# Where the modulation rows of two FFN layers stand in the instruction order: out of the gate/value tail and the down projection, into slots between the weight splits of the up projection

## The chip, the core and the metric

The kernel runs on one NeuronCore of a Trainium2 chip. The metric is the device time of one execution in microseconds (us). The engines of the core run their own instruction streams in order and meet at semaphores only: TensorE (PE) multiplies, VectorE (DVE) and ScalarE (ACT) do the elementwise work, GpSimd (POOL) helps, SyncE (SP) issues the transfers from HBM.

## The reference, cut to what matters

The program is a whole two-part network on 512 positions of width 1024. The first part has two layers, each a mixer and a convolutional FFN. The second part is modulated by a conditioning vector:

```python
def conv_ffn(x, w_up, conv_w, conv_b, w_down):          # D_FF = 2816
    gate, val = jnp.split(x @ w_up, 2, axis=-1)
    gp = jnp.pad(gate, ((0, 0), (CONV_WIDTH - 1, 0), (0, 0)))
    conv = conv_b
    for j in range(CONV_WIDTH):                          # 3 taps
        conv = conv + conv_w[j] * gp[:, j:j + s_]
    return (jax.nn.silu(conv) * val) @ w_down
...
# second part, layer i
shift, scale, gate = jnp.split((silu_c @ ada_w[i] + ada_b[i])[:, None, :], 3, axis=-1)
shift_c, scale_c, gate_c = jnp.split(silu_cc @ ada_w[i] + ada_b[i], 3, axis=-1)
```

`silu_c @ ada_w[i]` is a vector (1024) times a matrix (1024 x 3072). It depends on none of the first part's activations, so the kernel computes it beside the two FFNs: the modulation of second-part layer 0 (for two vectors, `silu_c` and `silu_cc`) beside `ffn(0)`, that of layer 1 (for one vector) beside `ffn(1)`.

## The kernel before, in words

All activations lie with the features on the 128 partitions and the 512 positions along the free axis. Weights come as one stream of chunks of 128 x 1024 floats, which are 8 tiles of 128 x 128. SP loads a chunk into one of 4 buffers `raw`. ACT rounds it to `whi` (L1176), DVE computes the rest `wlo = raw - whi` (L1780), each into one of 3 buffers. A projection multiplies each tile three times, `whi` by the high part, `whi` by the low part, `wlo` by the high part of the activation (L318, L321, L322). PE starts a chunk when its `wlo` is there (semaphore `w_lo`). ACT may write the `whi` of chunk c once PE has started chunk c - 1, because the buffer is that of chunk c - 3 and PE frees a chunk with the first matmul of the next (`w_used`).

An FFN has 22 feature blocks f, worked in two halves of 11. For each f, PE runs a gate projection (8 tiles, so one chunk, 24 matmuls) and a value projection (one chunk, 24 matmuls). DVE makes two `wlo` chunks per f and then does `tail(f)`: `gp` (L2045, out of PSUM), two convolution steps (L2049, L2052), the value (L2055), two products (L2057, L2060) and `hl` (L2064), the low part of the hidden block. ACT has a step between `gp` and L2049 (L1338), one after L2052 (a tanh, L1341) and one between L2060 and `hl` (L1345). Both engines' order is fixed by the program: the chunk splits (class `Ahead`) run up to two chunks ahead of the chunk that the program is at. DVE therefore makes in iteration f the `wlo` of the gate and the value of f + 1, in the order `wlo`, `wlo`, `tail(f)`.

After 11 blocks PE runs the down projection of that half: 8 output blocks of 11 tiles. Tile k of the first output block waits for `hl` of the k-th hidden block of the half.

The modulation is a generator `ada(layer)` on PE and one on DVE. It is advanced by `next(ad, None)` calls that stand between other work, so the number and the places of these calls and of the `yield`s in it set the order. The matrix comes as 24 rows of 128 x 1024 floats, `KD * g + k`, for three groups g of 8. For each row SP loads `aw` (3 buffers in layer 0, 2 in layer 1), and DVE adds `aw` times a scalar to `col` (L1998 for k = 0, L1995 else), twice per row in layer 0 (two vectors) and once in layer 1. After a group of 8 rows PE sums `col` over the partitions with 16 (layer 0) or 8 (layer 1) matmuls of one column each (L536) into bank 6. At the end DVE adds the bias (L2004) and forms the gains. `tiles.mark` in PE's generator sets where in the weight stream SP issues the load of a row.

In `ffn(1)` a second generator, `context()`, runs after `tail(f)` of f = 12 to 19: DVE multiplies a block of the context (L2027, left to POOL for k = 1, 4, 7), ACT shifts and rounds it, and DVE subtracts (L2029).

Of the kernel before, what the change touches and what calls it, by code (L numbers as in the profile page):

```python
# [13 lines left out]
MUL, ADD, SUB = ALU.mult, ALU.add, ALU.subtract  # L14
# [3 lines left out]
KD = 8  # L18
# [4 lines left out]
AW = 3, 2  # L23
# [69 lines left out]
def run(gen):  # L93
    for _ in gen:
        pass
# [180 lines left out]
HG_TILES = [0, 0, 3, 2, 2, 2, 2, 2, 2, 2, 1, 1, 1, 3, 0, 1]  # L276
MLA_BANKS = [{"tr0": 7, "tr1": 4, "qn": 5, "kn": 7, "knc": 4, "sg": 5}, {"qn": 7, "kn": 4, "knc": 5, "sg": 7}]
MLA_OUT_BANKS = [7, 4, 5, 3, 0, 1, 2, 6]
HIDDEN_AT = {(3, 2): 0, (4, 2): 1, (5, 2): 2}


# [27 lines left out]
def tensor_program(e, m, s):  # L309
    q = Waits(e)  # L310
    tiles = Tiles(q, s, m)
# [210 lines left out]
    def ada(layer):  # L522

        nv = 2 - layer
        b, col = B[6], m.ffn[layer].col
        for g in range(3):
            for k in range(KD):
                tiles.mark(("ada", layer, KD * g + k))
                yield
            q.wait_ge(*s.made_v.at("col", layer, nv - 1, KD * g + KD - 1))  # L530
            if g == 0:
                q.wait_ge(*(s.hid_lo.at("on", KD - 1) if layer else s.taken_v.at("o", KD - 1)))
            for v in range(nv):
                for j in range(8):
                    at = nv * (8 * g + j) + v
                    op = e.matmul(b[:, at:at + 1], col[:, v, 128 * j:128 * j + 128], ones[:, 0:1], start=True, stop=True)  # L536
            op.then_inc(*s.filled.tick("ada", layer, g))
            yield

    def ffn(layer):  # L540
        a = m.ffn[layer]
        site = ("n1", "n3")[layer]
        up, dn = f"up{layer}", f"down{layer}"
        hh, hl = [a.hh[:, i, :] for i in range(HF)], [a.hl[:, i, :] for i in range(HF)]
        before = ("w_out", "wo")[layer]
        ready0 = operands_ready(site)
        ad = ada(layer)

        def bank_free(half, f, j):
            b = (2 * f + j) % 6  # L550
            if f > half * HF + 2:
                return lambda: q.wait_ge(*s.taken_v.at("gv"[j], layer, f - 3))
            if half:
                return lambda: q.wait_ge(*s.h.at(dn, 0, {0: 6, 1: 7}.get(b, b)))
            if b < 4:
                return lambda: q.wait_ge(*s.h.at(before, 4 + b))
            if layer == 0:
                return lambda: q.wait_ge(*(s.made_v.at("S", KD - 1, 2) if b == 4 else s.taken_v.at("o", KD - 2)))
            return lambda: q.wait_ge(*s.made_a.at("pt", KD - 1, 2 + b - 4))

        def behind(f, j):
            if j == 0 and f == 0:
                return {7: summed(site, rb_read(("o", KD - 1)) if layer == 0 else lambda: q.wait_ge(*s.h.at("wo", 0)))}
            if j == 1 and f == 0:
                return {5: spread(site)}
            if layer == 1 and j == 0 and f == 11:
                def ready():
                    q.wait_ge(*s.acc.at("ctx", KD - 1))
                    q.wait_ge(*s.rb.at("n3"))
                return {3: sums("ctx", m.acc, 2, ready), 7: spread("ctx", n=2)}  # L570
            return {}

        for half in range(2):
            for f in range(half * HF, half * HF + HF):
                run(project(2 * f % 6, up, f, ("gate", layer, f), nhi, nlo, bank_free(half, f, 0),
                            ready0 if f == 0 else nothing, then=behind(f, 0)))
                run(project((2 * f + 1) % 6, up, FT + f, ("val", layer, f), nhi, nlo, bank_free(half, f, 1),
                            then=behind(f, 1)))
                if f > 1:
                    next(ad, None)  # L580

            def ready(k, half=half):
                q.wait_ge(*s.hid_lo.at("f", layer, half * HF + k))

            for i in range(KD):
                f0 = half * HF + HF - 3

                def free(i=i, f0=f0):
                    if i >= 6:
                        q.wait_ge(*s.h.at(dn, half, i - 6))  # L590
                        return
                    for f in range(f0, f0 + 3):
                        for j in range(2):
                            if (2 * f + j) % 6 == i:
                                q.wait_ge(*s.taken_v.at("gv"[j], layer, f))
                run(project(i % 6, dn, i, (dn, half, i), hh, hl, free, ready, ks=HF, k0=half * HF))
                if half == 0:
                    next(ad, None)

    def swa():  # L600
        a = m.swa
# [529 lines left out]

    hgrn()
    ffn(0)
    swa()
    ffn(1)
    mla()
    hyena()
# [635 lines left out]
def vector_program(e, m, s, chunks):  # L1773
    q = Waits(e)
# [205 lines left out]
    def ada(layer):  # L1980
        nv = 2 - layer
        ad, gs = m.ada[layer], m.gs[layer]
        bias = par[:, PC[f"ada_b{layer}"]:PC[f"ada_b{layer}"] + 24].unsqueeze(2).to_broadcast((128, 24, nv))
        col, aw = m.ffn[layer].col, m.ffn[layer].aw

        for g in range(3):
            for k in range(KD):
                n = KD * g + k
                q.wait_ge(*s.ada_w[n % AW[layer]].at(layer, n))
                if k == 0 and g:  # L1990
                    q.wait_ge(*s.filled.at("ada", layer, g - 1))
                for v in range(2):
                    if v < nv and k:
                        q.wait_ge(*s.made_v.at("col", layer, v, n - 1))
                        e.scalar_tensor_tensor(col[:, v, :], aw[:, n % AW[layer], :], m.scv[:, 2, k, v:v + 1], col[:, v, :],  # L1995
                                               MUL, ADD).then_inc(*s.made_v.tick("col", layer, v, n))
                    elif v < nv:
                        e.tensor_scalar(col[:, v, :], aw[:, n % AW[layer], :], m.scv[:, 2, k, v:v + 1], None,  # L1998
                                        MUL).then_inc(*s.made_v.tick("col", layer, v, n))
                    yield  # L2000
            yield
            yield
        q.wait_ge(*s.filled.at("ada", layer, 2))
        e.tensor_tensor(ad[:, 0:24, 0:nv], B[6][:, 0:24 * nv].rearrange("p (m v) -> p m v", v=nv), bias,  # L2004
                        ADD).then_inc(*s.ada_o.tick(layer))
        gain = par[:, PC[f"norm_g{layer}"]:PC[f"norm_g{layer}"] + 8].unsqueeze(2).to_broadcast((128, KD, nv))
        q.wait_ge(*s.ada_o.at(layer))
        e.tensor_scalar(gs[:, :, 0:nv], ad[:, 8:16, 0:nv], 1.0, None, ADD).then_inc(*s.setup_v.tick("gs1", layer))
        q.wait_ge(*s.setup_v.at("gs1", layer))
        e.tensor_tensor(gs[:, :, 0:nv], gs[:, :, 0:nv], gain, MUL).then_inc(*s.setup_v.tick("gs2", layer))  # L2010
        if layer == 0:
            q.wait_ge(*s.setup_v.at("gs2", 0))
            e.tensor_tensor(gs[:, :, 0], gs[:, :, 0], par[:, PC["final_norm"]:PC["final_norm"] + 8],
                            MUL).then_inc(*s.setup_v.tick("gs3"))
# [17 lines left out]
    def ffn(layer):  # L2032
# [5 lines left out]
        ad = ada(layer)  # L2038
        side = context() if layer else iter(())

        def tail(f):
# [1 line left out]
            q.wait_ge(*s.filled.at("gate", layer, f))  # L2043
            q.wait_ge(*s.rb.at(site))
            e.tensor_tensor(gp[:, z, 2:T + 2], B[2 * f % 6], m.rb[:, :], MUL).then_inc(*s.taken_v.tick("g", layer, f))  # L2045
            if f > 1:
                next(ad, None)
            q.wait_ge(*s.made_a.at("c0", layer, f))
            e.scalar_tensor_tensor(t[:, 2, z, :], gp[:, z, 1:T + 1], pc(cw, 22 + f), t[:, 0, z, :], MUL,  # L2049
                                   ADD).then_inc(*s.made_v.tick("c1", layer, f))  # L2050
# [7 lines left out]
                                   MUL).then_inc(*s.made_v.tick("s2", layer, f))  # L2058
            q.wait_ge(*s.made_v.at("s2", layer, f))
            e.tensor_tensor(t[:, 3, z, :], t[:, 0, z, :], t[:, 3, z, :], MUL).then_inc(*s.made_v.tick("mo", layer, f))  # L2060
            if f > 1:
                next(ad, None)
            q.wait_ge(*s.hid_hi.at("f", layer, f))
            e.tensor_tensor(a.hl[:, i, :], t[:, 3, z, :], a.hh[:, i, :].bitcast(F),  # L2064
                            SUB).then_inc(*s.hid_lo.tick("f", layer, f))
# [1 line left out]
        for half in range(2):  # L2067
            for f in range(half * HF, half * HF + HF):
                for k in range(KD):
                    w.tiles(1)  # L2070
                    if f == 0 and k == 7:
                        root(site, m.rc)
                    if layer and f == 11 and k == 3:
                        root("ctx", a.rcc, 2)
                if f == 1:
                    tail(0)
                run(w.steps(KD))
                if f:
                    tail(f)
                if f > 1:  # L2080
                    next(side, None)
            for i in range(KD):
                run(w.steps(HF))
                if half == 0:
                    next(ad, None)
                    next(ad, None)
                residual(i % 6, i, (dn, half))
                if half and layer == 0:
                    lo_scaled("n2", i, pc("attn_norm", i))
# [851 lines left out]
```

## Time and profile before

| quantity | us |
|---|---|
| median of 3 runs (2130.52 to 2132.89) | 2131.46 |
| the profiled execution's own time | 2130.52 |
| its span, first to last instruction | 2128.7 |
| PE busy | 2032.9 |
| DVE busy | 1360.7 |
| ACT busy | 807.0 |

The profiled execution is the fastest of the three. 1.8 us of its own time lie outside the span. The mean granted TensorE clock is 0.984 of full speed. Matmuls overlap in their pipeline, so their listed durations (about 390 ns) are longer than the distance from one to the next; the starts in a timeline tell how fast PE goes.

### The profile page before, as it was taken

The page shows a single profiled execution, that of the slowest core. Times are in us where ns is not written, and L with a number is a line of the kernel's source. Part 1 is how long each engine was busy: PE and PEld are TensorE (multiplying, and loading weights), DVE is VectorE, ACT ScalarE, POOL GpSimd, SP SyncE. Part 2 cuts the span into 40 slices and gives each one's busy share as a digit, 9 for nine tenths or more (in the row PEclk, how much of TensorE's full clock was granted, in tenths as well). Part 3 has the DMA queues.
Part 4 walks back from the last instruction along what each step waited for, and adds up shares of the span by engine and source line. Part 5 has one row for each costly group of instructions (what it writes and reads, how often), then busy time and mean ns, then how long its engine had stood idle before and what let it go on. Part 6 is the DMA issues. An engine that isn't in the chain of part 4 may idle for free.

```text
span 2128.7 us, 24442 instructions
## 1 busy us (share of the span) xinstructions
PE 2032.9 (95%) x9814; PEld 1657.6 (78%) x9814; DVE 1360.7 (64%) x1937; ACT 807.0 (38%) x1236; POOL 234.2 (11%) x239
## 2 busy tenths in 40 slices
PE   8999999999999989999999999999999799999887
PEld 6888887888888878888888887777776576768676
DVE  4577766875684566567648745544445678787774
ACT  4333334331333445444324434333333343444342
POOL 2133321000000100100000011000001213120201
PEclk9999999999999999999999999999999899999998
DMA  5211113434332300234443323111001222233221
GB/s 183 71 50 51 59 50 100 158 121 159 132 128 83 104 31 31 70 137 148 150 139 129 119 89 109 50 40 40 31 30 62 82 73 94 79 105 100 74 89 50
DMA packets 55009, 191.61 MB, mean 90 GB/s; under 512 B 6000, under 2 KB 6320, under 8 KB 54768
## 3 DMA queue, kind: packets, MB, share of 16 engines
q1 hardware_dynamic: 54896, 190.04, 26.6%
q8 instruction: 78, 1.28, 0.2%
q14 instruction: 35, 0.29, 0.0%
HBM read 187.92 MB, written 2.10 MB: 89 GB/s over the span
## 4 chain that ended last, share of the span: by engine, by line
PE 76%; DVE 15%; ACT 5%; issue 2%; POOL 2%; DMA 0%; SPq 0%; DVEq 0%; ACTq 0%
PE PS L318 20%; PE PS L322 19%; PE PS L321 19%; DVE wlo L1780 2%; PE PS L430 2%; PE PS L890 2%; PE PS L864 2%; PE PS L865 2%; PE PS L325 2%; PE PS L328 2%; PE PS L329 2%; ACT s_s L1406 1%; PE PS L879 1%; PE PS L380 1%; DVE s_s L2117 1%
## 5 line engine op out<-in xcount | busy, mean ns | idle before, releaser
L318 PE MATMUL PS<-nhi,whi 128*128 128x512 f32 x1456 | 601.4, 413 | 25.4 <-DVE nlo L1817 8.5
L322 PE MATMUL PS<-nhi,wlo 128*128 128x512 f32 x1456 | 574.0, 394 | 0.0
L321 PE MATMUL PS<-nlo,whi 128*128 128x512 f32 x1456 | 573.3, 394 | 0.0
L1780 DVE TENSOR_TENSOR wlo<-raw,whi 128x1024 fp32r<-128x1024 f32 x291 | 361.7, 1248 | 231.5 <-ACT whi L1176 230.9
L1176 ACT ACTIVATE whi<-raw 128x1024 fp32r<-128x1024 f32 x291 | 304.2, 1052 | 197.7 <-PE PS L318 180.7
L318 PEld LDWEIGHTS PS<-nhi,whi 128*128 128x128 f32 x1456 | 277.3, 190 | 97.2 <-issue 18.4
L322 PEld LDWEIGHTS PS<-nhi,wlo 128*128 128x128 f32 x1456 | 276.8, 190 | 60.5
L321 PEld LDWEIGHTS PS<-nlo,whi 128*128 128x128 f32 x1456 | 277.6, 191 | 52.9 <-issue 2.6
L2578 POOL TENSOR_TENSOR diag<-diag,sqb 128x512 f32<-128x512 f32 (+1 forms) x56 | 73.3, 1309 | 1175.3 <-ACT sqb L1185 1092.9
L318 PE MATMUL PS<-hh_f,whi 128*128 128x512 f32 x352 | 138.2, 393 | 0.0
L322 PE MATMUL PS<-hh_f,wlo 128*128 128x512 f32 x352 | 137.9, 392 | 0.0
L321 PE MATMUL PS<-hl_f,whi 128*128 128x512 f32 x352 | 137.9, 392 | 0.0
L1824 DVE TENSOR_TENSOR hT<-hT,PS 128x512 f32<-128x512 f32 x48 | 32.9, 685 | 92.7 <-PE PS L322 92.7
L1560 ACT ACTIVATE pt_m<-PS 128x768 f32<-128x768 f32 x32 | 26.0, 813 | 157.5 <-PE PS L879 157.5
L1995 DVE SCALAR_TENSOR_TENSOR col_f<-aw_f,scv,col_f 128x1024 f32<-128x1024 f32 x63 | 79.9, 1277 | 0.0
L318 PEld LDWEIGHTS PS<-hh_f,whi 128*128 128x128 f32 x352 | 66.8, 190 | 14.0
L322 PEld LDWEIGHTS PS<-hh_f,wlo 128*128 128x128 f32 x352 | 66.6, 189 | 14.0
L321 PEld LDWEIGHTS PS<-hl_f,whi 128*128 128x128 f32 x352 | 66.7, 189 | 13.8
L2291 DVE TENSOR_REDUCE sm_m<-PS 128x1 f32<-128x768 f32 x32 | 30.6, 956 | 62.9 <-PE PS L865 62.9
L1338 ACT ACTIVATE t_f<-gp_f,par 128x512 f32<-128x512 f32 x44 | 35.9, 817 | 85.4 <-DVE gp_f L2045 85.4
L430 PEld LDWEIGHTS PS<-qa,kk 128*128 128x128 f32 x448 | 56.0, 191 | 14.3 <-DVE qa L1932 10.3
L1185 ACT ACTIVATE sqb<-hT 128x512 f32<-128x512 f32 x42 | 26.3, 629 | 107.0 <-DVE hT L1824 70.3
(344 smaller groups left out, 3360.0 us busy)
## 6 DMA issues: line engine op xcount, KB each, us to landing
raw<-in_stream SPq DMA_DIRECT2D x291, 512.0 KB, 3.5
aw_f<-in_ada SPq DMA_DIRECT2D x48, 512.0 KB, 4.4
dc<-in_decay SPq DMA_DIRECT2D x4, 1024.0 KB, 5.5
hT<-in_xT SPq DMA_DIRECT2D x8, 256.0 KB, 7.3
out<-hT SPq DMA_DIRECT2D x8, 256.0 KB, 2.0
ctx_f<-in_ctx SPq DMA_DIRECT2D x1, 1024.0 KB, 6.8
ab_h<-in_filt_out SPq DMA_DIRECT2D x8, 128.0 KB, 2.9
mask<-in_masks SPq DMA_DIRECT2D x1, 512.0 KB, 8.7
```

Source lines behind the costliest of these rows:

```text
L318: op = e.matmul(out, hi, xh, start=first, stop=False)
L321: e.matmul(out, hi, xl, start=False, stop=False)
L322: return e.matmul(out, lo, xh, start=False, stop=last)
L325: op = e.matmul(out, xh, w[0], start=first, stop=False, skip_group_check=skip)
L328: e.matmul(out, xh, w[1], start=False, stop=False, skip_group_check=skip)
L329: return e.matmul(out, xl, w[0], start=False, stop=last, skip_group_check=skip)
L430: op = e.matmul(B[b][:, cs], kk[:, z, cs], qx[:, cs], start=True, stop=True)
L864: e.matmul(b[:, 0:n], a.qn[:, z, c], a.kn[:, z, ks], start=True, stop=False)
L1176: e.activation(m.whi[:, c % HL, :], m.raw[:, c % RAW, :], ACT.Copy).then_inc(*s.w_hi.tick(c))
L1780: e.tensor_tensor(m.wlo[:, c % HL, :], m.raw[:, c % RAW, :], m.whi[:, c % HL, :].bitcast(F), SUB).then_inc(*s.w_lo.tick(c))
L1995: e.scalar_tensor_tensor(col[:, v, :], aw[:, n % AW[layer], :], m.scv[:, 2, k, v:v + 1], col[:, v, :], MUL, ADD).then_inc(*s.made_v.tick(" ...
L2578: e.tensor_tensor(acc, acc, m.sqb[:, i % 2 if site != "n4" else 0, 0:width], ADD).then_inc(*s.acc.tick(site, i))
```

## The change

The rows of the modulation are placed by a table, `ADA_AT`, of 12 slots per group, of which 8 hold a row. Both generators now begin with three empty slots. In the up projection there are two slots per f (one in f = 0), the first behind the gate projection, the second behind the value projection. The slots inside `tail(f)` and in the down projection are gone. In layer 0 a slot of DVE now holds both vectors of a row.

```diff
+ADA_AT = [None, None, 0, 1, 2, 3, None, 4, 5, 6, 7, None]
...
         b, col = B[6], m.ffn[layer].col
+        for _ in range(3):
+            yield
         for g in range(3):
-            for k in range(KD):
-                tiles.mark(("ada", layer, KD * g + k))
+            for k in ADA_AT:
+                if k is not None:
+                    tiles.mark(("ada", layer, KD * g + k))
                 yield
             q.wait_ge(*s.made_v.at("col", layer, nv - 1, KD * g + KD - 1))
...
             op.then_inc(*s.filled.tick("ada", layer, g))
-            yield
...
                 run(project(2 * f % 6, up, f, ("gate", layer, f), nhi, nlo, bank_free(half, f, 0),
                             ready0 if f == 0 else nothing, then=behind(f, 0)))
+                next(ad, None)
                 run(project((2 * f + 1) % 6, up, FT + f, ("val", layer, f), nhi, nlo, bank_free(half, f, 1),
                             then=behind(f, 1)))
-                if f > 1:
+                if f:
                     next(ad, None)
...
-                if half == 0:
-                    next(ad, None)
...
+        for _ in range(3):
+            yield
         for g in range(3):
-            for k in range(KD):
...
-                    yield
-            yield
-            yield
+            for k in ADA_AT:
+                if k is not None:
+                    row(g, k)
+                yield
+        yield
         q.wait_ge(*s.filled.at("ada", layer, 2))
...
             e.tensor_tensor(gp[:, z, 2:T + 2], B[2 * f % 6], m.rb[:, :], MUL).then_inc(*s.taken_v.tick("g", layer, f))
-            if f > 1:
-                next(ad, None)
...
             e.tensor_tensor(t[:, 3, z, :], t[:, 0, z, :], t[:, 3, z, :], MUL).then_inc(*s.made_v.tick("mo", layer, f))
-            if f > 1:
-                next(ad, None)
...
                 if f == 1:
                     tail(0)
+                next(ad, None)
                 run(w.steps(KD))
                 if f:
+                    next(ad, None)
                     tail(f)
...
                 run(w.steps(HF))
-                if half == 0:
-                    next(ad, None)
-                    next(ad, None)
                 residual(i % 6, i, (dn, half))
```

`row(g, k)` holds the waits and the one or two DVE instructions of a row, unchanged. The placement of both versions, the same in both layers:

| | group 0 | group 1 | group 2 |
|---|---|---|---|
| before: rows | one per f, f = 2 to 9 | one per output block of the first down projection | one per f, f = 12 to 19 |
| before: PE's one-column matmuls | behind f = 10 | behind f = 11 | behind f = 20 |
| after: rows | f = 3 to 7 (2, 2, 1, 2, 1) | f = 9 to 13 (2, 2, 1, 2, 1) | f = 15 to 19 (2, 2, 1, 2, 1) |
| after: PE's one-column matmuls | in f = 8, behind the gate | in f = 14, behind the gate | in f = 20, behind the gate |

On DVE in layer 0, one iteration of f (here f = 4). `wlo` is a weight split, `col_f` the modulation, `gp_f` to `hl_f` the tail. Before:

```order
L2064 TENSOR_TENSOR hl_f<-t_f,hh_f 128x512
L1780 TENSOR_TENSOR wlo<-raw,whi 128x1024 x2
L2045 TENSOR_TENSOR gp_f<-PS,rb 128x512
L1995 SCALAR_TENSOR_TENSOR col_f<-aw_f,scv,col_f 128x1024
L2049 SCALAR_TENSOR_TENSOR t_f<-gp_f,par,t_f 128x512
L2052 SCALAR_TENSOR_TENSOR t_f<-gp_f,par,t_f 128x512
L2055 TENSOR_TENSOR t_f<-PS,rb 128x512
L2057 SCALAR_TENSOR_TENSOR t_f<-t_f 128x512
L2060 TENSOR_TENSOR t_f<-t_f 128x512
L1995 SCALAR_TENSOR_TENSOR col_f<-aw_f,scv,col_f 128x1024
L2064 TENSOR_TENSOR hl_f<-t_f,hh_f 128x512
```

The same iteration after, where it holds two rows of the matrix:

```order
L1782 TENSOR_TENSOR wlo<-raw,whi 128x1024
L1997 SCALAR_TENSOR_TENSOR col_f<-aw_f,scv,col_f 128x1024 x2
L1782 TENSOR_TENSOR wlo<-raw,whi 128x1024
L1997 SCALAR_TENSOR_TENSOR col_f<-aw_f,scv,col_f 128x1024 x2
L2052 TENSOR_TENSOR gp_f<-PS,rb 128x512
L2054 SCALAR_TENSOR_TENSOR t_f<-gp_f,par,t_f 128x512
L2057 SCALAR_TENSOR_TENSOR t_f<-gp_f,par,t_f 128x512
L2060 TENSOR_TENSOR t_f<-PS,rb 128x512
L2062 SCALAR_TENSOR_TENSOR t_f<-t_f 128x512
L2065 TENSOR_TENSOR t_f<-t_f 128x512
L2067 TENSOR_TENSOR hl_f<-t_f,hh_f 128x512
```

Four `col_f` instructions stand in front of `gp_f` where two stood inside the tail, and none stands between `gp_f` and the first convolution step or in front of `hl_f` any more.

On PE in layer 0, the change from the up projection of the first half (operand `nhi`) to the down projection (operand `hh_f`). Before:

```order
L318 MATMUL PS<-nhi,whi 128x512
L321 MATMUL PS<-nlo,whi 128x512
L322 MATMUL PS<-nhi,wlo 128x512
L536 MATMUL PS<-ones,col_f 128x1 x16
L318 MATMUL PS<-hh_f,whi 128x512
```

The group of one-column matmuls after, now in the middle of f = 8:

```order
L319 MATMUL PS<-nhi,whi 128x512
L322 MATMUL PS<-nlo,whi 128x512
L323 MATMUL PS<-nhi,wlo 128x512
L540 MATMUL PS<-ones,col_f 128x1 x16
L319 MATMUL PS<-nhi,whi 128x512
L322 MATMUL PS<-nlo,whi 128x512
```

It left the boundary between the two projections and stands between a gate and a value projection.

On DVE in layer 1, around a context step (`tmc_f`, `call`) in the second half. Before:

```order
L2064 TENSOR_TENSOR hl_f<-t_f,hh_f 128x512
L2027 TENSOR_TENSOR tmc_f<-ctx_f,rbc_f 128x256
L2029 TENSOR_TENSOR call<-tmc_f,call 128x256
L1780 TENSOR_TENSOR wlo<-raw,whi 128x1024 x2
L2045 TENSOR_TENSOR gp_f<-PS,rb 128x512
L1995 SCALAR_TENSOR_TENSOR col_f<-aw_f,scv,col_f 128x1024
L2049 SCALAR_TENSOR_TENSOR t_f<-gp_f,par,t_f 128x512
```

After, in an iteration with two rows:

```order
L2067 TENSOR_TENSOR hl_f<-t_f,hh_f 128x512
L2034 TENSOR_TENSOR tmc_f<-ctx_f,rbc_f 128x256
L2036 TENSOR_TENSOR call<-tmc_f,call 128x256
L1782 TENSOR_TENSOR wlo<-raw,whi 128x1024
L1997 SCALAR_TENSOR_TENSOR col_f<-aw_f,scv,col_f 128x1024
L1782 TENSOR_TENSOR wlo<-raw,whi 128x1024
L1997 SCALAR_TENSOR_TENSOR col_f<-aw_f,scv,col_f 128x1024
L2052 TENSOR_TENSOR gp_f<-PS,rb 128x512
L2054 SCALAR_TENSOR_TENSOR t_f<-gp_f,par,t_f 128x512
```

Here too the row left the place behind `gp_f`, and a second row joined it.

## Rows read from the trace of the kernel before

**Rows 1.** The page's chain of waits by engine, and PE's waits from 343 to 700 us

```profile
PE 76%; DVE 15%; ACT 5%; issue 2%; POOL 2%; DMA 0%; SPq 0%; DVEq 0%; ACTq 0%
...
PE PS L318 <- DVE nlo L1800: 0.2, 1, 0.2
```

**Rows 2.** Busy time of the engines (PE, PEld, DVE, ACT, POOL) in the first up projection

```profile
343.00:464.00 121.00, 120.79 (x548) 100.04 (x547) 96.47 (x119) 46.61 (x59) 0.06 (x1) 1.00 0.40 140
```

**Rows 3.** Timeline of DVE, layer 0, f = 5: start, duration, instruction, idle time before it

```profile
402.29 1.23 DVE L1780 TENSOR_TENSOR wlo<-raw,whi 128x1024 fp32r<-128x1024 f32 x1 [1.36 <-ACT whi L1176]
403.43 0.68 DVE L2045 TENSOR_TENSOR gp_f<-PS,rb 128x512 f32<-128x512 f32 x1
404.03 1.27 DVE L1995 SCALAR_TENSOR_TENSOR col_f<-aw_f,scv,col_f 128x1024 f32<-128x1024 f32 x1
405.22 0.74 DVE L2049 SCALAR_TENSOR_TENSOR t_f<-gp_f,par,t_f 128x512 f32<-128x512 f32 x1
...
409.99 0.68 DVE L2064 TENSOR_TENSOR hl_f<-t_f,hh_f 128x512 fp32r<-128x512 f32 x1
...
414.31 0.69 DVE L2045 TENSOR_TENSOR gp_f<-PS,rb 128x512 f32<-128x512 f32 x1
```

**Rows 4.** Timeline of DVE, layer 0, f = 1 to 2, without modulation

```profile
362.89 0.68 DVE L2045 TENSOR_TENSOR gp_f<-PS,rb 128x512 f32<-128x512 f32 x1
364.46 0.75 DVE L2049 SCALAR_TENSOR_TENSOR t_f<-gp_f,par,t_f 128x512 f32<-128x512 f32 x1 [0.89 <-ACT t_f L1338]
...
368.82 0.69 DVE L2064 TENSOR_TENSOR hl_f<-t_f,hh_f 128x512 fp32r<-128x512 f32 x1 [0.70 <-ACT hh_f L1345]
369.77 2.36 DVE L1780 TENSOR_TENSOR wlo<-raw,whi 128x1024 fp32r<-128x1024 f32 x2 [0.26 <-ACT whi L1176]
372.05 0.68 DVE L2045 TENSOR_TENSOR gp_f<-PS,rb 128x512 f32<-128x512 f32 x1
```

**Rows 5.** Timeline of DVE, two modulation rows (both vectors) in the down projection

```profile
468.11 1.41 DVE L1998 TENSOR_SCALAR col_f<-aw_f,scv 128x1024 f32<-128x1024 f32 x2
...
476.81 2.48 DVE L1995 SCALAR_TENSOR_TENSOR col_f<-aw_f,scv,col_f 128x1024 f32<-128x1024 f32 x2
```

**Rows 6.** Timeline of PE at one-column groups and in the down projection, layer 0

```profile
460.55 4.32 PE L536 MATMUL PS<-ones,col_f 128*128 128x1 f32 x32
...
474.19 0.39 PE L318 MATMUL PS<-hh_f,whi 128*128 128x512 f32 x1
...
538.11 3.63 PE L536 MATMUL PS<-ones,col_f 128*128 128x1 f32 x32
541.60 0.62 PE L318 MATMUL PS<-nhi,whi 128*128 128x512 f32 x1
```

**Rows 7.** Timeline of DVE at the ends and starts of halves, layer 0

```profile
463.74 0.69 DVE L2064 TENSOR_TENSOR hl_f<-t_f,hh_f 128x512 fp32r<-128x512 f32 x1 [0.69 <-ACT hh_f L1345]
...
535.39 0.68 DVE L2045 TENSOR_TENSOR gp_f<-PS,rb 128x512 f32<-128x512 f32 x1
...
551.50 0.69 DVE L2045 TENSOR_TENSOR gp_f<-PS,rb 128x512 f32<-128x512 f32 x1
```

**Rows 8.** Timeline of DVE, layer 1, second half, f = 11, 15 and 16

```profile
1104.75 0.68 DVE L2045 TENSOR_TENSOR gp_f<-PS,rb 128x512 f32<-128x512 f32 x1
...
1150.80 0.68 DVE L2045 TENSOR_TENSOR gp_f<-PS,rb 128x512 f32<-128x512 f32 x1
...
1160.04 2.36 DVE L1780 TENSOR_TENSOR wlo<-raw,whi 128x1024 fp32r<-128x1024 f32 x2 [0.34 <-ACT whi L1176]
1162.31 0.68 DVE L2045 TENSOR_TENSOR gp_f<-PS,rb 128x512 f32<-128x512 f32 x1
...
1170.35 2.36 DVE L1780 TENSOR_TENSOR wlo<-raw,whi 128x1024 fp32r<-128x1024 f32 x2 [0.53 <-ACT whi L1176]
```

**Rows 9.** Busy share by microsecond (PE, PEld, DVE, ACT, POOL), granted clock, DMA share, GB/s

```profile
465.00:466.00 1.00, 1.00 (x3) 0.81 (x3) 0.00 (x0) 0.12 (x1) 0.00 (x0) 0.50 0.00 0
...
770.00:771.00 1.00, 0.00 (x0) 0.00 (x0) 0.17 (x1) 0.99 (x4) 0.00 (x0) 1.00 0.00 0
```

More of the change, by code:

```diff
@@ L1984, in ada, with row @@
         col, aw = m.ffn[layer].col, m.ffn[layer].aw
-        for g in range(3):
-            for k in range(KD):
[L1988 to L1999, printed above, removed]
-                    yield
-            yield
-            yield
+        def row(g, k):
+            n = KD * g + k
+            q.wait_ge(*s.ada_w[n % AW[layer]].at(layer, n))
+            if k == 0 and g:
+                q.wait_ge(*s.filled.at("ada", layer, g - 1))
+            for v in range(nv):
+                c = m.scv[:, 2, k, v:v + 1]
+                if k:
+                    q.wait_ge(*s.made_v.at("col", layer, v, n - 1))
+                    op = e.scalar_tensor_tensor(col[:, v, :], aw[:, n % AW[layer], :], c, col[:, v, :], MUL, ADD)
+                else:
+                    op = e.tensor_scalar(col[:, v, :], aw[:, n % AW[layer], :], c, None, MUL)
+                op.then_inc(*s.made_v.tick("col", layer, v, n))
+        for _ in range(3):
+            yield
+        for g in range(3):
+            for k in ADA_AT:
[3 more added lines that the diff above has]
+        yield
         q.wait_ge(*s.filled.at("ada", layer, 2))
```

## The prediction

> **What bounds the kernel now.** I read the chain of waits first: three quarters of it is PE, and from 343 to 700 us, which is all of `ffn(0)`, PE waited 0.2 us [rows 1]. Then the busy times of an up projection: PE has 120.8 of 121 us, DVE 96.5 [rows 2]. So PE is the bound, and DVE has 20% to spare. How much of that a rearrangement may use is told by DVE's timeline. In steady state one f takes 10.88 us from `gp` to `gp` [rows 3], which is PE's pace for 48 matmuls (0.2267 each). DVE idles 1.36 us of it, and this idle is all that it has in front of a weight split. The `col` instructions cost little there, since they stand where DVE would wait for ACT: without them it idles 0.89 us behind `gp` and 0.70 us in front of `hl` [rows 4], with them it idles at neither place [rows 3]. The reader is to see both timelines side by side: the tail from `gp` to the end of `hl` takes 6.62 us without and 7.24 us with two `col` [rows 3, 4], so two instructions of 1.27 us cost 0.62 us.
>
> **What is removed, and what moved instructions cost.** No instruction is added or removed; the order shows them moved, so a change that does nothing is out. I keep two clocks. DVE's, when it runs behind: 9.16 us per f without modulation (372.05 - 362.89, [rows 4]), plus what stands in the new slots, where nothing of ACT's is hidden. A row of both vectors is 2.39 there (2.48 less 0.09 of overlap: a `col` starts 1.19 before its successor though it lasts 1.27, [rows 3]), the first of a group 1.33 [rows 5]. So an f with two rows takes 13.94 us, with one 11.55, with none 9.16, against PE's 10.88. Six f with eight rows need 9.16 x 6 + 1.33 + 7 x 2.39 = 73.0 us; PE needs 65.3 and 3.49 for the one-column group (541.60 - 538.11, [rows 6]), 68.8. So in layer 0 DVE becomes the bound of the up projection.
>
> How long PE doesn't notice: the next gate's `wlo` is the first thing behind a tail, done 8.2 us after `gp` (6.62, 0.26 idle, one split, [rows 4]). In steady state PE starts gate f at 13.6 us after `gp` of f - 2: gate 10 starts at 460.55 - 10.88 = 449.67 [rows 6], `gp` of f = 8 at 414.31 + 21.76 = 436.07 [rows 3]. The difference, 5.4 us, is what `gp` may be late.
>
> **Layer 0, first half.** From `gp` of f = 2 at 372.05 the sums give 384.9, 398.9, 410.4, 424.4, 435.9, 445.1, 458.0 and 471.9 for f = 3 to 10 (two rows, two, one, two, one, none, 1.33 + 2.39, two). The pace of before is 381.67 + 10.88 per f, so lateness is 3.3, 6.3, 7.0, 10.1, 10.7, 9.0, 11.0, 14.1. Gate 6 waits 0.9, gate 7 brings it to 1.6, gate 8 to 4.7; there the one-column group follows, so gates 9 and 10 wait no more. The end of the half binds harder. Tile 10 of the first down block needs `hl` of f = 10, that is 471.9 + 6.6 = 478.5, and a semaphore: 478.6. Before, `hl` was there at 464.4 [rows 7] and PE reached this tile at 474.19 (the 31st triple behind the group, [rows 6]), with 3.4 us lost to a low clock on the way (460.55 + 3.49 + 30 x 0.2267 = 470.8 without it). What the clock does in f = 8 now doesn't count, since `hl` is later anyway. Cost: **+4.4**.
>
> **Layer 0, second half.** `gp` of f = 11 stands at 535.39 before [rows 7]; one row in front makes it 2.4 late. Then 5.5 (f = 12), 6.1, 0.9 in f = 14, where the group gives DVE 3.5 us, 2.4 (its own row at least), 5.5, 6.1, 9.2 in f = 18, 9.9. Gate 20 waits 9.2 - 5.4 = 3.8; behind it stands the third group, which covers f = 19's lateness. `gp` 21 is 3 to 4 late, less than PE by now. Cost: **+3.8**.
>
> **Layer 1, first half.** One `col` per row, 1.20 in a slot and 0.7 for the first of a group. Two rows make 11.56, one 10.36: lateness 1.4, 2.1, 1.6, 2.2, 1.7, 0, 1.2, 1.9. Nothing over 5.4, and `hl` of f = 10 has 2.9 us before the down tile wants it (as in layer 0: 460.55 + 6.8 - 464.43, [rows 6, 7]). Cost: **0**.
>
> **Layer 1, second half.** Here the context step stands behind the tail. It makes f take 11.52 from f = 15 to 16 and 10.3 from 16 to 17, where POOL has its part (1162.31 - 1150.80 and 1170.35 + 2.27 - 1162.31, [rows 8]), with one `col` inside the tail, which adds 0.22 (half of a pair that hides nearly as well; 11.30 and 10.09 without). The next gate's split is done 10.5 us after `gp` with a full context step (1160.04 + 1.2 - 1150.80), 9.3 without, so slack is 3.1 or 4.3. From 1104.75 + 1.2 for f = 11 [rows 8]: lateness 1.2, 1.9, 3.5, 1.1 (group, 1.75), 3.4, 6.2, 6.7, 9.5, 11.1 for f = 11 to 19. Gate 18 waits 1.9, gate 19 brings it to 3.6, gate 20 to 9.5 - 3.1 = 6.4; f = 19 asks for 11.1 - 4.3 - 1.75 = 5.1, less. Cost: **+6.4**.
>
> **What costs nothing.** The rows left the down projection, where DVE idled more than half; PE gains nothing there, since it waited for nothing. The loads: a row needs the `col` of three (layer 1: two) rows earlier, which stands at least two weight splits ahead in DVE's order, and lands long before its slot; SP waits for that `col` with the next weight chunk behind it, but that chunk is used three chunks later. Were this wrong, a chunk would come late by one `col`, 1.3 us, once or twice. The bias step now comes before `tail(20)`, 0.6 us of DVE, in the sums above. PE's wait for the 8th row of a group comes a whole f behind it. The same three groups of 16 matmuls are issued; a stretch at half clock followed each (granted 0.50 at 465 us, [rows 9]). I expect it again, at 1.7 to 3.4 each, in new places, and count no difference.
>
> **Sum.** 4.4 + 3.8 + 0 + 6.4 = +14.6 on the profiled execution's 2130.5, 2145.1; the median of the runs is 0.9 above it, so I say 2145.5. The bounds: the 4.4 is firm, being one chain of DVE instructions against one PE time. If PE bears more lateness than 5.4 elsewhere, the others shrink to 0: 2135. If DVE's waits for ACT grow by 0.3 per f in the lagging stretches (the 0.26 idle of [rows 4] twice), each half gains 2 us: 2151.
>
> **The rivals.** (a) *The waits themselves lower the clock.* PE would stand for up to 3 us in front of gates 8 and 20. For it: what is behind a one-column group ran at half clock. Against it: at 770 us PE is idle for the whole microsecond and the clock stays 1.00 [rows 9]. Price: two further stretches of 2.6 (the mean of 1.7 and 3.4), the one of the first half being hidden by `hl`: 2150.
> The Trainium skill ("TensorE: Matmul & The Clock Gate", section "HAM oscillation — how this bites in real kernels") says that waits of PE between bursts of matmuls bring the half-rate clock back, whose price comes on top of the wait. It speaks against this change, and by it the time is the 2150 of (a). The row at 770 us doesn't bear it out for a wait this short; the groups of one-column matmuls, in which PE never idles, do lower it here.
> (b) *DVE's lateness stays within the buffers after the first half.* PE's starts would bend with DVE's, ACT giving back time. For it: in layer 1 `gp` of f = 16 was 1.4 late before (1162.31 against 1104.75 + 1.75 + 5 x 10.88, [rows 8]) and the chain of waits shows DVE at 15% only [rows 1]. Against it: the sums pass the slack by 3.8 and 6.4. Time: 2135, or 2131 if the first half too is smaller.
> (c) *Faster.* Taken off the boundary, the groups are followed by a dense up projection and no stretch at half clock comes; before they cost 3.4, 1.7 (551.50 - 535.39 - 10.88 - 3.49, [rows 7]) and, taken like the first, 3.4, together 8.5. It decides if DVE's lateness at gate 8 stays under 5.4 and at `hl` of f = 10 under the 2.9 + 3.5 of slack; then the time is 2130.5 - 8.5 = 2122. Against it: the second group already stood in a dense up projection and lost clock.
>
> **How the numbers follow.** The forecast has 0.70, (a) 0.13, (b) 0.11, (c) 0.06. About 0.2%, 4.3 us, is what a measurement of this kernel tells from no change. The forecast's own range is 2141 to 2149. With (a) and the upper part of (b) 2135 to 2151 leaves out under 2 in 10. Slower holds the forecast, (a) and a part of (b), 0.86; same the rest of (b), 0.09; faster 0.05.
>
> **What would show it.** `gp` to `gp` of 13.9 us in f = 4, 6 and 10 of layer 0, with idle times of 0.88 and 0.70 in every tail; PE waiting for `wlo` in front of gates 6 to 8, 20, and in layer 1 18 to 20, 15 to 18 us in all with the wait for `hl` of f = 10; no such wait in layer 1's first half. DVE busy as before in sum. Wrong would be: `gp` of f = 10 before 468 us, PE waiting at none of these gates, or a granted clock that is 1.00 behind the groups.

## The result, and the profile after

| | before | after |
|---|---|---|
| median of 4 runs, us | 2132.18 (2130.52 to 2133.66) | 2154.16 (2149.54 to 2155.59) |
| profiled execution, us | 2130.52 | 2150.94 |
| its span, us | 2128.7 | 2148.8 |
| granted clock | 0.984 | 0.982 |
| DVE busy, us | 1360.7 | 1364.1 |

The ratio of the times is 1.0105, 95% interval 1.0085 to 1.0127: slower by 22 us, or 20.4 by the two profiled executions. All six executions on record of the kernel after lie between 2149.54 and 2159.31. The forecast was slower by 14.6, with a range that ended at 2151. The direction and the places are right, the size is not.

The view of waits of the kernel after, for PE in `ffn(0)` and then in `ffn(1)` (waiter, what it waited for, us in total, times, longest), answers to the 0.2 us of [rows 1]:

```profile
PE PS L319 <- DVE wlo L1782: 6.9, 5, 2.7
PE PS L319 <- DVE hl_f L2067: 2.4, 1, 2.4
...
PE PS L319 <- DVE wlo L1782: 5.0, 3, 2.5
```

In all 14.3 us, 8 of the 9 waits for a weight split and one for `hl` of f = 10. Of the first line 3.8 us are at gates 6, 7 and 8, the rest at gates 19 and 20; those of the last line are at layer 1's gates 18, 19 and 20 (a wait at gate f is one in front of the gate projection of block f). DVE's timeline of f = 4 and 5 shows why, in the place of [rows 3]:

```profile
396.11 2.48 DVE L1997 SCALAR_TENSOR_TENSOR col_f<-aw_f,scv,col_f 128x1024 f32<-128x1024 f32 x2
398.50 0.69 DVE L2052 TENSOR_TENSOR gp_f<-PS,rb 128x512 f32<-128x512 f32 x1
400.07 0.75 DVE L2054 SCALAR_TENSOR_TENSOR t_f<-gp_f,par,t_f 128x512 f32<-128x512 f32 x1 [0.88 <-ACT t_f L1340]
...
404.43 0.69 DVE L2067 TENSOR_TENSOR hl_f<-t_f,hh_f 128x512 fp32r<-128x512 f32 x1 [0.70 <-ACT hh_f L1347]
405.38 2.36 DVE L1782 TENSOR_TENSOR wlo<-raw,whi 128x1024 fp32r<-128x1024 f32 x2 [0.26 <-ACT whi L1178]
407.66 2.47 DVE L1997 SCALAR_TENSOR_TENSOR col_f<-aw_f,scv,col_f 128x1024 f32<-128x1024 f32 x2
410.05 0.68 DVE L2052 TENSOR_TENSOR gp_f<-PS,rb 128x512 f32<-128x512 f32 x1
```

The `col` pairs now stand in front of `gp`, and the 0.88 and 0.70 us that they used to cover are idle again, as where no modulation ran [rows 4]. DVE is as busy as before in sum, but not at the same moments.

Where the time went, by the starts of the same instruction in both timelines: 0.35 us less ahead of `ffn(0)` (`gp` of f = 0 at 354.53, before 354.88), then 16.0 us in layer 0 (layer 1's first `gp` at 943.96, before 928.29), 5.9 in layer 1 up to its second down projection (1241.61, before 1220.00), and 1.5 less in the rest.

PE at gate 8 and at the tile that waits for `hl` of f = 10, in the place of [rows 6]:

```profile
432.13 0.79 PE L319 MATMUL PS<-nhi,whi 128*128 128x512 f32 x1 [2.75 <-DVE wlo L1782]
432.71 0.63 PE L322 MATMUL PS<-nlo,whi 128*128 128x512 f32 x1
...
482.70 0.50 PE L319 MATMUL PS<-hh_f,whi 128*128 128x512 f32 x1 [2.44 <-DVE hl_f L2067]
```

The second of these matmuls is one of 0.63 us, where 0.39 is usual. The granted clock says the same (busy share of PE, PEld, DVE, ACT, POOL; then the clock), behind gate 8 and behind the one-column block of f = 8:

```profile
433.00:434.00 1.00, 1.00 (x4) 0.71 (x4) 1.00 (x2) 0.00 (x0) 0.00 (x0) 0.50 0.77 139
...
443.00:449.00 6.00, 6.00 (x16) 4.75 (x16) 3.61 (x5) 1.87 (x2) 0.00 (x0) 0.50 0.72 249
```

Half clock, that is 1.2 GHz, from 432.2 to 435.6 and again from 442.4 to 449.2, which holds all of 443 to 449. And DVE, which was late, now waits for PE in the tail of f = 8. In front of it stands a weight split that waited for ACT's `whi`, and ACT waited for PE to free the buffer:

```profile
444.00 1.06 ACT L1178 ACTIVATE whi<-raw 128x1024 fp32r<-128x1024 f32 x1 [1.64 <-PE PS L319]
...
445.08 1.23 DVE L1782 TENSOR_TENSOR wlo<-raw,whi 128x1024 fp32r<-128x1024 f32 x1 [1.47 <-ACT whi L1178]
446.23 0.68 DVE L2052 TENSOR_TENSOR gp_f<-PS,rb 128x512 f32<-128x512 f32 x1
...
451.74 0.69 DVE L2060 TENSOR_TENSOR t_f<-PS,rb 128x512 f32<-128x512 f32 x1 [2.41 <-PE PS L323]
...
481.95 0.69 DVE L2067 TENSOR_TENSOR hl_f<-t_f,hh_f 128x512 fp32r<-128x512 f32 x1 [0.69 <-ACT hh_f L1347]
```

### The profile page after: what moved, and what is told of

It reads as the page before. It is cut to its first block, busy times and chain, and to the rows that moved or that the text cites. A ratio compares the mean times of both kernels' runs of the same rounds, so it can differ in the third digit from the quotient of the medians.

```text
span 2148.8 us, 24444 instructions
## 1 busy us (share of the span) xinstructions
PE 2039.9 (95%) x9814; PEld 1660.5 (77%) x9814; DVE 1364.1 (63%) x1937; ACT 804.3 (37%) x1236; POOL 234.3 (11%) x239
## 4 chain that ended last, share of the span: by engine, by line
PE 68%; DVE 20%; ACT 7%; issue 3%; POOL 2%; DMA 0%; SPq 0%; DVEq 0%; ACTq 0%
PE PS L319 17%; PE PS L323 17%; PE PS L322 17%; DVE wlo L1782 4%; PE PS L431 2%; PE PS L892 2%; PE PS L866 2%; PE PS L867 2%; PE PS L326 2%; DVE col_f L1997 2%; PE PS L330 2%; PE PS L329 2%; ACT whi L1178 2%; ACT s_s L1408 1%; PE PS L881 1%
## 5 line engine op out<-in xcount | busy, mean ns | idle before, releaser
L431 PEld LDWEIGHTS PS<-qa,kk 128*128 128x128 f32 x448 | 56.0, 191 | 14.3 <-DVE qa L1934 10.4
```

The costliest lines, as they stand in the source:

```text
L431: op = e.matmul(B[b][:, cs], kk[:, z, cs], qx[:, cs], start=True, stop=True)
```

## The experiments

Theory A: the rows in front of `gp` make DVE late, PE waits, and a slow stretch of the clock in f = 8 holds DVE back in turn, so that `hl` of f = 10 comes later than DVE's own work says. Rivals: B, the new places of the one-column blocks cost the time; C, the clock follows PE's waits alone; D, the rate of two rows per f decides, wherever the rows stand. Each kernel was timed beside the kernel before on the same chip (19 and 22 runs, medians 2132.31 and 2133.58).

**Rows back in the tail, all else as after.**

```diff
-                next(ad, None)
                 run(w.steps(KD))
                 if f:
-                    next(ad, None)
                     tail(f)
...
                 # in tail(f)
+            next(ad, None)
             q.wait_ge(*s.made_a.at("c0", layer, f))
...
+            if f:
+                next(ad, None)
             q.wait_ge(*s.hid_hi.at("f", layer, f))
```

> The kernel after with PE's order and the number of rows per f unchanged, but DVE's two slots back inside the tail, one behind gp and one in front of hl, where DVE waits for ACT. Theory A (the place decides: in front of gp a row hides nothing): an f with two rows takes 12.4 us of DVE instead of 13.9 and six f 66.9 against PE's 68.8, gp is never over 5.4 us late, PE waits at no gate: 2131 to 2134 us. Rival D (the rate of two rows per f decides, wherever they stand): 2146 to 2154.

2131.22 us, ratio 0.9993 (0.9978 to 1.0007): the whole loss is gone within that interval, with PE's order and the rate of two rows per f unchanged. PE's waits in `ffn(0)`:

```profile
PE PS L319 <- DVE nlo L1802: 0.2, 1, 0.2
```

DVE's timeline of this kernel, f = 4 and 5:

```profile
398.63 2.48 DVE L1997 SCALAR_TENSOR_TENSOR col_f<-aw_f,scv,col_f 128x1024 f32<-128x1024 f32 x2
401.02 0.69 DVE L2070 TENSOR_TENSOR hl_f<-t_f,hh_f 128x512 fp32r<-128x512 f32 x1
...
403.89 0.68 DVE L2052 TENSOR_TENSOR gp_f<-PS,rb 128x512 f32<-128x512 f32 x1
```

`gp` of f = 5 stands at 403.89, in the kernel after at 410.05. An f with two rows took DVE 11.8 us, where 12.4 was expected and after takes 13.9. Rivals B and D fall: the blocks and the rate are those of after.

**Before's schedule, but the two steps of an f in front of `gp`.**

```diff
                 # in tail(f), twice
-            if f > 1:
-                next(ad, None)
...
                 run(w.steps(KD))
+                if f > 1:
+                    next(ad, None)
+                    next(ad, None)
                 if f:
                     tail(f)
```

> The kernel before, its schedule (one row per f, rows in the down projection, blocks at the old places) unchanged, but the two steps of an f in one place in front of gp instead of inside the tail. Theory A (place): layer 0 takes 11.55 us of DVE per f against 10.88, lateness grows by 0.67 per f to 7.3 at f = 9, PE waits 1 to 2 us in each half; layer 1's second half takes 12.5 and 11.3 per f, lateness reaches 10 and PE waits about 5.8 us: in all + 8.5, 2140.8 us. Rival D (the rate of two rows per f): no change, 2132.

2139.13 us, ratio 1.0023 (1.0013 to 1.0033). Slower by 4.9, where 8.5 was expected: the place alone costs, at half the rate. PE waited 0.6 us in front of gates 9 and 10 of `ffn(0)` (and once more for 0.1), and in `ffn(1)` 3.4 us in three waits for a weight split, the longest 1.3.

The 1 to 2 us of each half of layer 0 were too much, and so was layer 1's 5.8. By the starts in the two profiles `ffn(0)` is as long as before (363.9 us in both from its first `gp` to the end of its second down projection, here with 3.4 us less of half clock), and layer 1 is 4.8 us longer up to its second down projection. So the place alone costs in layer 1; in layer 0 the loss of after needs the place and the rate together.

**The change in layer 0 alone.** PE's and DVE's generators take `ADA_AT` and the new calls in layer 0 and before's in layer 1, which then has before's order on every engine:

```diff
-            for k in ADA_AT:
+            for k in (range(KD) if layer else ADA_AT):
...
-                next(ad, None)
+                if not layer:
+                    next(ad, None)
```

> The change in layer 0 alone; layer 1 has the order of before on every engine. By after's trace layer 0 costs 15.6 us and layer 1's second half 5: 2132.3 + 15.6 = 2147.9 us, with waits of PE in front of gates 6, 7, 8, 19 and 20 and for hl of f = 10, and none in ffn(1). Were the two layers' costs tied (layer 1 started late or in another clock phase), it would be under 2144 or as slow as after, 2153.

2151.16 us, ratio 1.0074 (1.0058 to 1.009), 15.8 us, as expected by the ratio. The medians differ by 17.6; the six runs lie between 2144.15 and 2152.95. The profiled one is the fastest: its `ffn(0)` has the waits of after (6.9 and 2.4 us) and costs 11.5 instead of 16. In its up and down projections the clock was at half for 17.1 us, in after's for 27.3, and half of the difference, 5.1, is near the 4.5 that it saved. Among others the wait for `hl` and the wait of 2.74 in front of gate 8 left the clock alone:

```profile
431.00:432.00 1.00, 1.00 (x6) 0.80 (x5) 1.00 (x2) 0.00 (x0) 0.00 (x0) 1.00 0.57 111
```

So the same order of instructions can cost 11.5 or 16 us in layer 0, by what the clock does.

**The second vector of layer 0 cut to 8 columns.**

```diff
-                    op = e.scalar_tensor_tensor(col[:, v, :], aw[:, n % AW[layer], :], c, col[:, v, :], MUL, ADD)
+                    r = slice(0, 8 if v else 1024)
+                    op = e.scalar_tensor_tensor(col[:, v, r], aw[:, n % AW[layer], r], c, col[:, v, r], MUL, ADD)
```

> The kernel after with the second vector's accumulation of layer 0 cut to 8 of 1024 columns (rows k = 1 to 7; part of the modulation of the context is left out), so that a row costs DVE 1.3 instead of 2.4 us in layer 0; PE's instructions are those of after. Theory A: no wait of PE in layer 0; only layer 1's second half keeps its 5 us: 2136 to 2138 us. Rival B (the blocks' new places): 2148 to 2154, since they and their places are unchanged.

2140.30 us, ratio 1.0034 (1.0022 to 1.0047). PE waits for nothing in the up projections of `ffn(0)`, though PE has after's blocks in after's places there; in `ffn(1)` it waits as in after, three times for a weight split, 5.0 us in all.

The median is 2.3 us above the range that was expected. 1.3 of it have a name: here the wait of 2.51 in front of layer 1's gate 20 was followed by six matmuls at half clock, which in after's profile it was not. The rest is open. Rival B falls a second time.

**One-column matmuls spread over 8 tiles**, in the kernel after and in the kernel before:

```diff
-            for v in range(nv):
-                for j in range(8):
-                    at = nv * (8 * g + j) + v
-                    op = e.matmul(b[:, at:at + 1], col[:, v, 128 * j:128 * j + 128], ones[:, 0:1], start=True, stop=True)
-            op.then_inc(*s.filled.tick("ada", layer, g))
+            def piece(j, g=g):
+                for v in range(nv):
+                    at = nv * (8 * g + j) + v
+                    op = e.matmul(b[:, at:at + 1], col[:, v, 128 * j:128 * j + 128], ones[:, 0:1], start=True, stop=True)
+                if j == 7:
+                    op.then_inc(*s.filled.tick("ada", layer, g))
+            pending.update({j: lambda j=j: piece(j) for j in range(8)})
...
                 # the next projection runs pending[k] behind its tile k
-                            then=behind(f, 1)))
+                            then=beside(behind(f, 1))))
```

> The kernel after, with the one-column matmuls of a group no longer in one block: 2 of them (layer 1: 1) behind each of the first 8 tiles of the projection that follows. DVE's order is that of after. Theory A (DVE is late and PE waits; the waits and the blocks both halve the clock; a block's slow stretch in f = 8 holds DVE's tail of f = 8 back, so that the end of the half moves too): hl of f = 10 comes 4.1 us earlier, the slow stretches behind the blocks of f = 14 and 20 (1.5 and 1.9 us) go: about 2146.5 us against a median of 2154 of after (2143.5 against its profile), the waits in front of gates 6 to 8, 20 and layer 1's 18 to 20 stay. Rival B (the blocks' new places cost the time, not DVE): 2132 or less. Rival C (the clock follows PE's waits alone): 2154, no change against after.

2150.09 us, ratio 1.0079 (1.0063 to 1.0095): by the two ratios 5.5 us better than after, where 7.6 were expected. The two intervals reach 3.4 and 4.5 us to each side, so that by the times alone this gain isn't clear of noise. The waits stayed, at 0.70, 0.36, 2.73, 2.44, 0.33, 2.76 and layer 1's three. Up to layer 1's second down projection it is 7.9 us ahead of after in the profiles, of which 6.1 are lost in later stages, which the change doesn't touch. Behind the wait at gate 8 PE ran at half clock here too (431.8 to 438.0), with no block before it. Rival C falls: the stretches behind the blocks are gone. Its other half stands: waits lower the clock too.

> The kernel before, with its one-column matmuls spread in the same way over the 8 tiles that follow. Theory A: PE waits for nothing in the FFNs and the slow stretches behind layer 0's three blocks (3.4, 1.7 and about 3.4 us) go: 2132.2 - 8.5 = 2123.7 us, granted clock 1.00 from 344 to 700 us. Rival C (the clock falls for another reason than the blocks): 2132. A third way: a lone one-column matmul among wide ones costs more than one in a block (0.11 us): each 0.1 us more would add 7 us: 2131.

2127.02 us, ratio 0.9967 (0.9953 to 0.9981): 7 us faster than before, where 8.5 was expected, and the lowest ratio here. The granted clock from 344 to 700 us is 1.00, in the kernel before 0.98:

```profile
344.00:700.00 356.00, 356.00 (x1616) 295.88 (x1617) 249.80 (x291) 119.17 (x145) 6.50 (x5) 1.00 0.37 129
```

PE's timeline shows the pairs, with the three wide matmuls of a tile between them; a block of 16 took 3.49:

```profile
461.05 0.50 PE L545 MATMUL PS<-ones,col_f 128*128 128x1 f32 x4
...
462.19 0.50 PE L545 MATMUL PS<-ones,col_f 128*128 128x1 f32 x4
```

A tile with its pair takes 1.14 us and one without 0.68, so 8 pairs cost 3.7: no cheaper than the block. The gain is all clock: `ffn(0)` is 7.7 us shorter in the profile, and before ran 17.1 us of it at half clock. Layer 1, whose blocks of eight were spread too, gained nothing.

**Both together: rows in the tail, one-column matmuls spread.**

> Rows inside the tail at two per f (as after_tail) and the one-column matmuls spread over 8 tiles (as before_split). Both parts act apart: PE waits at no gate, no half clock in the FFNs, as fast as before_split, 2127 us (2124 to 2129). If the rows at this rate need the blocks' 3.5 us for DVE to catch up, PE waits in front of a gate after f = 7: 2130 or more.

2128.50 us, ratio 0.9980 (0.9969 to 0.9991), with no wait of PE for DVE in the FFNs but the 0.2 us that before has too, and no half clock in the projections of `ffn(0)`. Its interval overlaps that of the kernel before with the spread alone, so with rows in the tail neither schedule is shown to be better. It also overlaps that of the rows in the tail without the spread.

**The step that failed, by itself: 2 instead of 16 one-column matmuls in layer 0's groups.**

```diff
-                for j in range(8):
+                for j in range(8 if layer else 1):
```

> The kernel after with 2 instead of 16 one-column matmuls in each of layer 0's three groups (the modulation of second-part layer 0 is mostly left out). Measures the step that failed: DVE's chain with PE not slow in f = 8. Theory A: DVE never waits for the value projection of f = 8, gp to gp is 9.15 from 7 to 8 and 12.87 from 8 to 9, hl of f = 10 ends at 478.2 instead of 482.65 us; the wait in front of gate 8 and a slow stretch behind it stay; the blocks' 9.2 us and the slow stretches behind them (up to 7 us) go, of which the first block's are partly hidden by DVE's lateness: 2154 - 12 = 2142 us. If hl of f = 10 stays at 482, something other than the block holds DVE.

2147.42 us, ratio 1.0064 (1.0051 to 1.0078). The total is 5 above the expectation (4 by the ratio). The second half waits three times (2.76, 0.37, 2.76) instead of twice, since without the block of f = 14 DVE has nothing to catch up in there; and the wait for `hl` of f = 10, 4.38 us, brought half clock. The step itself came out as expected, to a tenth of a us. `gp` of f = 8 and `hl` of f = 10, where `gp` of f = 0 stood at 352.82:

```profile
442.98 0.69 DVE L2052 TENSOR_TENSOR gp_f<-PS,rb 128x512 f32<-128x512 f32 x1
...
475.72 0.69 DVE L2067 TENSOR_TENSOR hl_f<-t_f,hh_f 128x512 fp32r<-128x512 f32 x1 [0.69 <-ACT hh_f L1347]
```

Four kernels with the same DVE order in layer 0's first half (all us; the last column is the end of `hl` 10 less the start of `gp` 0, for which the prediction's sum gives 478.5 - 354.9 = 123.6):

| kernel | `gp` 7 to 8 | tail of f = 8 | `gp` 8 to 9 | to the end of `hl` 10 |
|---|---|---|---|---|
| nearly no block, half clock for 3 us behind gate 8 | 9.15 | 6.62 | 12.88 | 123.6 |
| block with 3.4 us of half clock, full behind gate 8 | 9.14 | 7.31 | 14.26 | 125.0 |
| spread, half clock for 6 us behind gate 8 | 9.15 | 8.20 | 15.64 | 126.3 |
| block with 6.8 us of half clock, 3.4 us behind gate 8 (after) | 10.71 | 8.92 | 15.87 | 128.1 |

Each step that PE is slower in f = 8 is handed to DVE, and by DVE to the end of the half.

## Why the prediction was wrong

- **Right: what bounds.** The pace of DVE per f (13.93, 11.55 measured for 13.94, 11.55), the 0.88 and 0.70 idle in every tail, the waits at gates 6, 7, 8 (0.7, 0.4, 2.75; sum 3.8 for 4.7), none in layer 1's first half, layer 1's three waits (5.0) and its cost (5.9 for 6.4), and gates 19 and 20 of layer 0 (3.1 for 3.8).
- **Wrong: layer 0, first half, 4.4.** The step was "What the clock does in f = 8 now doesn't count, since `hl` is later anyway." It treated DVE as a chain that PE can't lengthen, and so called the 4.4 firm. But DVE needs PE in f = 8 in two ways, and PE had become late by the wait, the block, and the half clock behind both. The weight splits need ACT's `whi`, whose buffer PE frees: the first of two such waits made `gp` of f = 8 1.6 us late. The tail of f = 8 needs PE's value projection: 2.3 us. A second wait for `whi` makes most of the last 0.7. So `hl` of f = 10 came 4.5 us later than the sum (482.65 for 478.2 with the earlier start). The table shows that this is PE's slowness in f = 8: where PE had nearly no block there, the sum holds.
- **Wrong: rival (a) was counted as a rival, though it adds to the forecast.** The clock fell behind PE's wait at gate 8 (in the step above), behind the wait for `hl` (1.7 us, which was in no sum) and at gate 20 of layer 0. First half: 4.4 + 4.5 + 1.7 = 10.6, as measured. Second half: 3.8 expected, 5.4 measured. From one start of a matmul to the next, the two waits cost 3.4 there (3.1 as the view of waits lists them), half clock 1.2 more than in before, and 0.7 is spread over others. After was at half clock behind the block of f = 14, at gate 20 and behind the last block, before behind two blocks.
- **The upper bound.** 2151 came from longer waits of DVE for ACT in every f, and these did not grow: 0.88, 0.70 and 0.26 stayed, but for the two waits for `whi` in f = 8 and 9, which come from PE. It also took in (a)'s 2150, which has two stretches of half clock but not their path through DVE. The terms as measured are 10.6 + 5.4 + 5.9 = 21.9, less the 1.9 gained ahead of and behind the FFNs; the spans differ by 20.1. The forecast also has a slip of addition: 2145.1 and the 0.9 that it names make 2146.0, not 2145.5.
- **Why (a) had only 0.13.** The Trainium skill ("TensorE: Matmul & The Clock Gate", section "HAM oscillation — how this bites in real kernels") says that waits between bursts bring the half-rate clock back. The traces agree, for most waits and not for all: of 17 waits in the FFNs of 2.4 us or more, in five profiles, 10 had half clock from inside the wait or within 1.1 us of its end, 7 of 9 of 2.7 us, 2 of 7 (2.4 to 2.5), and the one of 4.4. The prediction set (a) aside by one row at full clock, at 770 us in before [rows 9]. That row is part of a wait of 2.62 us, and the same wait was followed by half clock in 8 of the 10 profiles here; before's is one of the two exceptions. In after, in the columns of [rows 9]:

```profile
788.00:789.00 1.00, 1.00 (x7) 1.00 (x6) 0.00 (x0) 1.00 (x6) 0.00 (x0) 0.50 0.08 16
```

- Rival (b) is out, since layer 0's second half and layer 1 waited. So is (c); the block at f = 8 was followed by half clock too.

The stages behind the FFNs, where all engines have the same order in all these kernels, moved by -1.5 to +9 us against before's profile. This too is mostly clock: behind the last down projection after had 49.9 us of half clock, before 53.0, and before with the two steps in front of `gp` 72.9; what was left to the end took 847.6, 849.1 and 858.0. A part of the distance between 20.4 and 22 may be that.

What stays open: why one and the same wait lowers the clock in one execution and not in the next.

## What to carry to other kernels

Work moved off the bounding engine's path is free only where its engine would have waited: inside the tail two instructions of 1.27 us cost 0.62, in front of `gp` 2.39. When two engines feed each other, a sum for the late one alone is a lower bound: look for the step at which it reads the other's result, and add what the other loses there, clock included. Here a block of sixteen narrow matmuls was better cut up among wide ones, though they then cost as much; with blocks of eight nothing was gained. And one row at full clock is one draw: look for the same wait in more than one profile before a rival is set aside by it.

## What the runs showed of the hardware

Sixteen one-column matmuls in a row (3.5 us and more), with PE never idle, were followed by a stretch at 1.2 GHz each time in layer 0 (18 of 18 blocks, in six profiles), blocks of eight in layer 1 (1.7 us) never (21 of 21, in seven), and pairs among wide matmuls never (three profiles). Waits of PE of 2.73 to 2.76 us in the FFNs were followed by one in 7 of 9 cases, waits under 1.4 us there never. Such a stretch slows a 128x512 matmul from 0.23 to 0.43 us, from one start to the next. That a kernel with such waits spreads more from run to run is not shown: the change in layer 0 alone ran from 2144 to 2153 us, and on the same chip the kernel before, which has none of them in its FFNs, from 2129 to 2139.
